# Four more seven-product pairs, a new dealing of modulation units, and a weight sum made by an accumulating transfer

## What is computed

```python
mod = (silu_c @ w_mod[l] + b_mod[l]).reshape(B, N_MOD, D_MODEL)
mod_c = (silu_cc @ w_mod[l] + b_mod[l]).reshape(1, N_MOD, D_MODEL)
h = h + 0.5 * m[2][:, None] * _swiglu(_modulate(_rms(h, norm_w[l, 0]), m[0], m[1]),
                                      ffn1_w_gu[l], ffn1_w_down[l])
hc = hc + 0.5 * mc[2][:, None] * _swiglu(_modulate(_rms(hc, norm_w[l, 0]), mc[0], mc[1]), ...)

def _swiglu(x, w_gu, w_down):
    g, u = jnp.split(x @ w_gu, 2, axis=-1)
    return (jax.nn.silu(g) * u) @ w_down
```

## Time and profile before

| | us |
|---|---|
| median of three runs | 1628.92 |
| the profiled execution | 1629.36 |
| its span, first to last instruction | 1627.7 |
| PE busy | 1612.9 |
| DVE busy | 1272.3 |
| ACT busy | 690.1 |
| GpSimd busy | 84.7 |
| idle of PE before matmuls, in waits | 11.4 |

### The profile page before, as it was taken

One profiled execution on the slowest core, in us unless ns is written; L12 is line 12 of the kernel. 1 busy time (PEld: TensorE's weight loads), 2 busy tenths in 40 slices (PEclk: granted clock), 3 DMA queues, 4 the chain that ended last, 5 costly groups with the idle time before them and its releaser, 6 DMA issues.

```text
span 1627.7 us, 24207 instructions
## 1 busy us (share of the span) xinstructions
PE 1612.9 (99%) x9396; PEld 1404.6 (86%) x9396; DVE 1272.3 (78%) x1973; ACT 690.1 (42%) x1056; POOL 84.7 (5%) x149
## 2 busy tenths in 40 slices
...
GB/s 380 148 191 172 168 174 163 195 200 100 113 67 52 79 97 155 150 147 151 155 176 187 206 105 160 150 147 149 155 179 182 95 114 83 103 201 188 183 187 149
DMA packets 69613, 250.46 MB, mean 154 GB/s; under 512 B 7552, under 2 KB 8576, under 8 KB 69376
## 3 DMA queue, kind: packets, MB, share of 16 engines
...
## 4 chain that ended last, share of the span: by engine, by line
PE 92%; DVE 5%; DMA 2%; issue 1%; ACT 1%; DVEq 0%; POOLq 0%; ACTq 0%
PE ps L1699 27%; PE ps L1700 26%; PE ps L1701 26%; PE ps L1742 3%; PE ps L1790 2%; PE ps L1743 2%; DMA wm<-wmod 1%; PE ps L1792 1%; PE ps L2108 1%; PE ps L1851 1%; PE ps L2076 1%; DVE shared_b L998 1%; DVE wm L998 1%; DVE wlo L980 1%; PE ps L2090 0%
## 5 line engine op out<-in xcount | busy, mean ns | idle before, releaser
L980 DVE TENSOR_TENSOR wlo<-raw,whi 128x1024 fp32r<-128x1024 f32 x320 | 387.5, 1223 | 191.7 <-ACT whi L546 188.9
L1699 PE MATMUL ps<-xh,whi 128*128 128x512 f32 (+1 forms) x1420 | 497.1, 350 | 2.7 <-DVE xl L1185 2.3
L1700 PE MATMUL ps<-xl,whi 128*128 128x512 f32 (+1 forms) x1420 | 489.1, 344 | 0.0
L1701 PE MATMUL ps<-xh,wlo 128*128 128x512 f32 (+1 forms) x1420 | 488.8, 344 | 0.0
L546 ACT ACTIVATE whi<-raw 128x1024 fp32r<-128x1024 f32 x320 | 335.6, 1056 | 354.6 <-PE ps L1701 269.1
L1699 PEld LDWEIGHTS ps<-xh,whi 128*128 128x128 f32 x1420 | 268.7, 189 | 41.2 <-DVE xl L1185 4.4
L1701 PEld LDWEIGHTS ps<-xh,wlo 128*128 128x128 f32 x1420 | 268.7, 189 | 32.6
L1700 PEld LDWEIGHTS ps<-xl,whi 128*128 128x128 f32 x1420 | 268.9, 189 | 32.3 <-issue 0.7
L1700 PE MATMUL ps<-al,whi 128*128 128x512 f32 (+2 forms) x768 | 263.8, 343 | 0.0
L1699 PE MATMUL ps<-ah,whi 128*128 128x512 f32 (+1 forms) x668 | 236.2, 354 | 4.7 <-DVE wlo L980 2.8
L1701 PE MATMUL ps<-ah,wlo 128*128 128x512 f32 (+1 forms) x668 | 235.5, 353 | 0.0
...
## 6 DMA issues: line engine op xcount, KB each, us to landing
...
wm<-wmod POOLq DMA_DIRECT2D x128, 512.0 KB, 4.8
...
```

What stands on the lines that cost most here:

```text
L980: dve.tensor_tensor(wlo[:, n % RING, :, :].rearrange("p a b -> p (a b)"), raw[:, n % RING, :], whi[:, n % SPL, :, :].rearrange("p a b -> p ...
L1699: pe.matmul(out_ap, hi_w, hi_x, start=start, stop=False)
L1700: pe.matmul(out_ap, hi_w, lo_x, start=False, stop=False)
L1701: return pe.matmul(out_ap, lo_w, hi_x, start=False, stop=stop)
```

## The change

SEVENS grows from 4, 8 and 8 pairs to 6, 9 and 9. The 32 units made within FFN 0 to 2 are dealt 12, 8 and 12 in place of 12, 11 and 9. Units from 28 on, which belong to modulations that only the latent stream uses, take one product; the context's columns are set to zero at the start. The sum up + gate is made by a transfer that GpSimd issues: it reads the first half of the gate block from DRAM again and adds it to the up block in `raw`. DVE then makes three sums, from that one, and DVE and ACT wait for the landing (`third_in`). GpSimd's loads, a loop before, are written out, and the accumulating transfer for pair j + 2 stands behind all loads that step j's turns free. The two halves of a seven-product pair's silu are cut by token half of the stream rather than by stream, and the two half-products become one.

```diff
-SEVENS = ((7, 11, 15, 19), (5, 7, 9, 11, 13, 15, 17, 19), (5, 7, 9, 11, 13, 15, 17, 19))
-MODS_GU = ({2: 1, 3: 1, 4: 2, 5: 2, 7: 2, 8: 2, 9: 2, 11: 2, 12: 2, 13: 2, 15: 2, 16: 2, 17: 2, 19: 2, 20: 2, 21: 1},
+UNIT_AT = {0: (4, 12), 1: (16, 8), 2: (24, 12)}
+X_ONLY = 28
+SEVENS = ((7, 9, 11, 14, 17, 19),
+          (4, 6, 8, 10, 12, 14, 16, 18, 20),
+          (4, 6, 8, 10, 12, 14, 16, 18, 20))
+MODS_GU = ({2: 1, 3: 1, 4: 2, 5: 3, 6: 1, 8: 2, 9: 1, 10: 2, 11: 1, 12: 3, 13: 1, 14: 1, 15: 3, 16: 1, 18: 2, 19: 2, 20: 2, 21: 2},
...
+MODS_DN = ({0: 1, 1: 1, 2: 1, 3: 1, 4: 1, 5: 1, 6: 1, 7: 1, 8: 1, 9: 1, 10: 2, 12: 1, 14: 1, 15: 1, 16: 1, 17: 1},
+           {0: 1, 1: 1, 2: 1, 3: 1, 5: 1, 6: 1, 7: 1, 8: 1, 9: 1, 10: 2, 13: 1, 14: 1, 15: 1, 17: 1},
+           {0: 1, 1: 2, 2: 2, 3: 1, 4: 2, 5: 2, 6: 1, 7: 2, 8: 2, 9: 2, 10: 3, 12: 2, 13: 1, 14: 2, 15: 1, 16: 2, 17: 1})
@@ GpSimd
+            def third_sum(f, j):
+
+                n = first_block(f) + 2 * j + 1
+                pool.wait_ge(raw_in[n % RING], 16 * (n // RING + 1))
+                pool.dma_start(raw[:, n % RING, 0:KQ * P], wstream[n - 1][:, 0:KQ * P], accum_op=ALU.add)\
+                    .then_inc(third_in, 16)
+
+            def ffn(f, m0):
+
+                made = m0
+                for j in range(FC):
+                    made += MODS_GU[f].get(j, 0)
+                    loads_to(u0 + 2 + made)
+                    if seven(f, j + 2):
+                        third_sum(f, j + 2)
@@ ACT, weight_sums_high
-                act.wait_ge(wsum_done, 4 * k + 2)
+                act.wait_ge(third_in, 16 * (k + 1))
                 split(n + 1)
@@ DVE, mod_pair
-                for v in range(2):
+                for v in range(2 if u < X_ONLY else 1):
@@ DVE, weight_sums
+                dve.wait_ge(third_in, 16 * (k + 1))
...
-                dve.tensor_tensor(s32[:, 0, :], up[:, 0:h], up[:, h:2 * h], ALU.add).then_inc(wsum_done, 1)
-                dve.tensor_tensor(up[:, 0:h], up[:, 0:h], gate[:, 0:h], ALU.add).then_inc(wsum_done, 1)
-                dve.wait_ge(wsum_done, 4 * k + 1)
-                dve.tensor_tensor(s32[:, 1, :], s32[:, 0, :], gate[:, 0:h], ALU.add).then_inc(wsum_done, 1)
-                dve.wait_ge(wsum_done, 4 * k + 3)
+                dve.tensor_tensor(s32[:, 1, :], up[:, 0:h], up[:, h:2 * h], ALU.add).then_inc(wsum_done, 1)
+                dve.wait_ge(wsum_done, 3 * k + 1)
+                dve.tensor_tensor(s32[:, 0, :], s32[:, 1, :], gate[:, 0:h], ALU.subtract).then_inc(wsum_done, 1)
                 dve.tensor_tensor(s32[:, 2, :], s32[:, 1, :], gate[:, h:2 * h], ALU.add).then_inc(wsum_done, 1)
```

More of the change, by code:

```diff
@@ L434, in seven, with first_block @@
             return f < 3 and j in SEVENS[f]
+        def first_block(f):
+            return (0, FFN + MIX, PER_LAYER)[f]
         def seventh(f, j):
@@ L494, in _, with loads_to @@
                 pool.dma_start(wm[:, c, :, :].rearrange("p a n -> p (a n)"), wmod[u0 + c]).then_inc(wm_in[c], 16)
-            def loads(a, b):
-                with pool.Fori(a, b) as i:
-                    for c in range(2):
-                        pool.wait_ge(wm_used, i * 2 + (c - 1 - u0))
-                        pool.dma_start(wm[:, c, :, :].rearrange("p a n -> p (a n)"),
-                                       wmod[bass.ds(i * 2 + c, 1)].rearrange("a p n -> p (a n)"))\
-                            .then_inc(wm_in[c], 16)
+            at = [u0 + 2]
+            def loads_to(end):
+                while at[0] < min(end, UNITS * PAIRS):
+                    q = at[0]
+                    pool.wait_ge(wm_used, q - 1 - u0)
+                    pool.dma_start(wm[:, q % 2, :, :].rearrange("p a n -> p (a n)"), wmod[q]).then_inc(wm_in[q % 2], 16)
+                    at[0] += 1
+            def third_sum(f, j):
[10 more added lines that the diff above has]
+                        third_sum(f, j + 2)
+                loads_to(u0 + 2 + made + sum(MODS_DN[f].values()))
+                return made + sum(MODS_DN[f].values())
             def zeros(l):
@@ L524, in conv_pool_low @@
                         .then_inc(cl_done, 1)
-            after_mix = (LATE_UNIT + 1) * PAIRS // 2 + 1
-            loads(u0 // 2 + 1, after_mix)
+            m1 = ffn(0, 0)
             zeros(0)
             conv_pool_low(0)
-            loads(after_mix, UNITS * PAIRS // 2)
+            m2 = ffn(1, m1)
+            ffn(2, m2)
             zeros(1)
@@ L591, in silu_seven @@
                 act.activation(ups[:, 0:S], ps[:, 7, 0:S], ACT.Copy).then_inc(s1_done, 1)
+                halves = sil[:, j % 2, :].rearrange("p (s h t) -> p s h t", s=2, h=2)
+                gates = first_up.rearrange("p (h s t) -> p h s t", h=2, s=2)
                 act.wait_ge(gate_a, k + 1)
-                act.activation(sil[:, j % 2, 0:S], first_up[:, 0:S], ACT.Silu).then_inc(silu_a, 1)
+                act.activation(halves[:, :, 0, :], gates[:, 0, :, :], ACT.Silu)
                 act.wait_ge(gate_b, k + 1)
-                act.activation(sil[:, j % 2, S:T], first_up[:, S:T], ACT.Silu).then_inc(silu_done, 1)
+                act.activation(halves[:, :, 1, :], gates[:, 1, :, :], ACT.Silu).then_inc(silu_done, 1)
             def ffn(l, st):
@@ L615, in ffn @@
                         x_sums_high()
-                    for c in HALVES_AT.get(j, ()):
+                    for c in HALVES_AT[f].get(j, ()):
                         hidden_high(f, c)
@@ L968, in _ @@
         def _(dve):
+            dve.memset(modc[:, X_ONLY // 2:, :, 1], 0.0)
             steps = [0]
@@ L1107, in seven_end @@
                 dve.tensor_tensor(first_up[:, S:T], two_ups[:, S:T], ps[:, 5, S:T], ALU.add).then_inc(gate_b, 1)
-                dve.tensor_tensor(pair_of(ups), twice(two_ups[:, 0:S]), last, ALU.add).then_inc(ups_done, 1)
+                dve.tensor_tensor(ups.rearrange("p (s h t) -> p h s t", s=2, h=2),
+                                  twice(two_ups[:, 0:S]).rearrange("p h (s t) -> p h s t", s=2),
+                                  last.rearrange("p h (s t) -> p h s t", s=2), ALU.add).then_inc(ups_done, 1)
             def seven_mul(f, j):
@@ L1113, in seven_mul @@
                 dve.wait_ge(ups_done, k + 1)
-                halves = hid[:, j * T:(j + 1) * T].rearrange("p (s h t) -> p s h t", s=2, h=2)
-                for i in range(2):
-                    if i:
-                        dve.wait_ge(silu_done, FC * f + j + 1)
-                    else:
-                        dve.wait_ge(silu_a, k + 1)
-                    ins = dve.scalar_tensor_tensor(halves[:, :, i, :],
-                                                   ups[:, i * S:(i + 1) * S].rearrange("p (s t) -> p s t", s=2), -1.0,
-                                                   sil[:, j % 2, i * S:(i + 1) * S].rearrange("p (s t) -> p s t", s=2),
-                                                   ALU.mult, ALU.mult)
-                ins.then_inc(mul_done, 1)
+                dve.wait_ge(silu_done, FC * f + j + 1)
+                dve.scalar_tensor_tensor(hid[:, j * T:(j + 1) * T], ups, -1.0, sil[:, j % 2, :], ALU.mult, ALU.mult)                    .then_inc(mul_done, 1)
             def gate_columns(m):
```

21 lines of the change are left out of this document (10 added, 11 removed).

## The result

The changed kernel takes 1649.53 us (median of four runs, 1645.75 to 1654.53) against 1628.78: a ratio of 1.0129 (95% interval 1.0102 to 1.0156), 20.7 us more where 9.8 more were forecast. The profiled execution is the fastest of the four, 1645.75 with a span of 1644.0.

The account below looks back on a forecast made before the run. PE, busy 1612.9 of 1627.7 us, was taken as the bound. Savings of 10.1 us against losses of 8.2 (FFN 0), 0.6 (FFN 1) and 11.1 (FFN 2) gave +9.8: 1639.2 profiled, 1638.7 median, range 1627 to 1651.

Parts of the forecast that it names:

- Four more pairs, -3.4: FFN 0 to 2: 24 seven-product pairs for 20, each saving 0.84 us of PE time, 3.4 us less.
- FFN 1's down projection, -6.7, and 0.6 back at its pair 21: FFN 1: fewer modulation turns remove PE's waits and slow clock, 6.7 us less; one added turn at pair 21 costs 0.6.
- The half-multiplications and the cut of the silu at nothing, and the transfer covered in the steady row up to a landing of 9.7: Seven-product pairs: DVE idles 3.03 us, so these edits cost nothing; on alternate pairs landings up to 9.7 us cost nothing.
- The transfer lands after 4.8 us (3.2 to 5.4): GpSimd's accumulating transfer: 4.8 us from issue to landing, ends 3.2 and 5.4, taken from a 512 KB load.
- Pair 7, 3.1: FFN 0 before pair 7: transfer queued behind the third turn's load, so PE waits 3.1 us (1.6 to 3.8).
- Pairs 14 and 17, 0.6 each (0 to 1.4): FFN 0: same pattern with three turns at steps 12 and 15, PE waiting 0.6 us each (0 to 1.4).
- The clock, 2.0 in FFN 0: FFN 0 behind the wait before pair 7: the lowered clock costs PE another 2.0 us.
- FFN 0's pair 21, 1.9: FFN 0's pair 21: two turns for one delay DVE's last product, 1.9 us lost.
- FFN 2's pair 21, 5.5 and 2.0 for the clock: FFN 2's pair 21: third turn waits for its load and delays the product, 5.5 us (5.0 to 6.3), plus 2.0 clock.
- FFN 2's block 15, 1.4, and its tail, 2.2: FFN 2's down projection: two buffers too slow for its turns, PE waiting 1.4 us at block 15, 2.2 for updates.
- rivals: Short landings, 1629.9 (chance 0.20); blocks in hand cover the waits, 1621.3 (0.15); slow accumulating transfer, 1694 (0.05).
- the third: Accumulating transfer lands beyond 9.7 us, every seven-product pair waits; at 12 us 55 us on the forecast, 1694; chance 0.05.

Follow-up runs that it names:

- re-dealt run: Changed kernel with units dealt 12, 10, 10, one turn at each FFN's pair 21 and FFN 0's accumulating transfer one load earlier: 1621.17 us, 0.9953 of before.
- The change again: The changed kernel run once more with no edit, to see the spread of its stages: 1651.59 us, 1.0132 of before.
- re-dealt run without the transfer: Units dealt 12, 10, 10 as in the re-dealt run, but the sum up + gate on DVE and no accumulating transfer: 1620.81 us, 0.9947 of before.
- run with the old dealing: Changed kernel with the 20 pairs, dealing and low halves' places of the kernel before, keeping the accumulating transfer: 1635.63 us, 1.0049 of before.

## Why the prediction was wrong in size

The direction and the places were right, and the time lies within the range (1627 to 1651), but the sum was half of what was measured: 9.8 us for 20.7. By its steps:

- **Four more pairs, -3.4.** Where no wait covers it, the gain shows: 1.6 in FFN 0's pairs (246.0 in the re-dealt run against 247.57), 0.8 in FFN 1's and 0.7 in FFN 2's of the changed kernel. 3.1 in all.
- **FFN 1's down projection, -6.7, and 0.6 back at its pair 21.** Right: -6.4 in the stage, with a wait of 0.4 at pair 21.
- **The half-multiplications and the cut of the silu at nothing, and the transfer covered in the steady row up to a landing of 9.7.** Right: landings of up to 6.2 us in FFN 1 and 2 left PE without a wait at their seven-product pairs in the first profile. The change again showed 0.4 at one of them, the re-dealt run without the transfer 0.5. How late a landing may be depends on the issue as well: the bound of 9.7 was worked out for a transfer issued 6.6 us after PE's start of the pair two before. In the run with the old dealing the one for FFN 1's pair 15 was issued 10.6 us after that start, and a landing of 7.4 cost the 0.9 us found there.
- **The transfer lands after 4.8 us (3.2 to 5.4).** This is the step that failed, in FFN 0: the term was too small, and the terms of pairs 14 and 17 and of the clock hang on it. The rows used were those of plain 512 KB loads, on the argument that bytes set the landing. With little beside it the accumulating transfer takes 4.1 us, where the plain one of its size takes 2.9. Behind a modulation load and beside a weight block it took 7.1, 6.2 and 5.5 for pairs 7, 14 and 17, and up to 7.6 in the change again. Without the addition it took 3.8, 3.8 and 4.4, near the term, and the three waits together 2.6 us in place of 8.6. The Trainium skill (Collectives: The Full Stack, "The bandwidth ceiling: the fold count and why AG ≠ RS ≠ AR") says of ReduceScatter that its add needs two source reads on one ring; the 1.2 us by which the landing fell without the addition have that sign, but no row here shows a second read. By the formula of the Trainium skill (DMA: Bandwidth & Descriptors, "Anatomy of one DMA — SWDGE (gpsimd) path") 256 KB take 2.6 us, an estimate; the plain transfer's 2.9 is near it and the accumulating one's 4.1 is not.
- **Pair 7, 3.1.** Measured 3.4, which is luck, since two errors cancel: the transfer was issued 2.8 us sooner than worked out (100.31 for 103.15), DVE having reached its turns 2.1 sooner, and landed 2.3 us later after issue.
- **Pairs 14 and 17, 0.6 each (0 to 1.4).** Measured 2.8 and 2.4. From PE's start of pair 12 (165.56) the transfer goes out at 15.0 where 14.3 was worked out, and lands at 21.3 where 19.1 was: 1.4 of the 2.2 missing us are the landing, 0.7 the issue. For pair 17, from the start of pair 15 (201.96), it goes out at 15.3 and lands at 20.8: of 1.8 missing us 0.7 are the landing and 1.0 the issue. DVE began these turns at 5.3 and 4.5, where 3.9 was worked out.
- **The clock, 2.0 in FFN 0.** It was charged once, and it was paid behind each of the three waits: 2.8 + 1.8 + 1.7 = 6.3. This 4.3 more and the 4.0 more of pairs 14 and 17 are 8.3 of the 8.8 us by which FFN 0 (waits 8.6, clock 6.3, 2.1 at pair 21: 17.0) exceeds the forecast's 8.2.
- **FFN 0's pair 21, 1.9.** Right: 2.1, and gone when its second turn moved away.
- **FFN 2's pair 21, 5.5 and 2.0 for the clock.** Right: 5.5 (5.2 to 6.2 in five more profiles), and a clock of 0.50 for 3.4 us, which is 1.7. Its third turn started at 1196.73, 6.24 behind the first, as the hop (the load is issued at 1192.07, 1.58 after the first turn's start) and the load's landing at 1196.64 want it; the hop was 0.4 shorter than the 1.94 taken and the landing 0.5 longer than the 4.1.
- **FFN 2's block 15, 1.4, and its tail, 2.2.** Right in mechanism, loose in size: 1.8 at block 15 and nothing in the tail in the first profile; 2.5 and 1.1 in the second. The sum for this stage was 11.1; the six profiles show 9.6 to 16.8. The prediction had said that this term runs from 0 to 12 with the landing of the loads, and that the upper ends together give 1650. The other runs do lie there or above (1648.19 to 1657.81), but not for that reason alone: in the change again FFN 0's terms came to 20.8, twice their upper end of 10.5, and FFN 2's to 15.0, under theirs of 20.4.

So the net of +9.8 was short by FFN 0's terms in the profiled execution (17.0 for 8.2; FFN 2 gave 1.5 less and the start 0.7), and by another 4.3 in the median, which the change again, as far as one profile can, puts down to FFN 0's landings and FFN 2's loads. That the time fell within the range owes something to luck: its upper end rested on FFN 2, and the excess came from FFN 0. None of the rivals came about, though the third had the sign right, since the accumulating transfer is slower than a plain one; the wait at every seven-product pair, which a landing above 9.7 us would have brought, was not seen.
